# Sparse attention: the weighing factor of unit s+1 ahead of the low parts of unit s in VectorE's list

## The reference, cut to what matters

```
for head h (16), for m in (0: selected blocks, 1: window):
    s = (q_rope[h] @ k_m.T) * 64**-0.5          # 512 x 512, causal
    p = softmax(s)
    o[h] += sigmoid(gate_logits)[h, 1 + m] * (p @ v_m)
o[h] += sigmoid(gate_logits)[h, 0] * o_compressed[h]
```

## Time and profile before

| | us |
|---|---|
| median of 3 runs | 2101.65 (2101.18 to 2110.67) |
| the profiled execution | 2101.01 |
| its span in the profile | 2099.2 |
| first transpose of unit 0 to first transpose of unit 31 | 241.94 |

### The profile page before, as it was taken

How to read it: one execution, slowest core, us unless ns; L and a number is a source line. 1 busy time by engine, 2 the same in 40 slices (tenths; PEclk the granted TensorE clock), 3 DMA queues, 4 the chain that set the end, 5 groups by cost and what they waited for, 6 DMA issues and landing times.

```text
span 2099.2 us, 25667 instructions
## 1 busy us (share of the span) xinstructions
PE 2016.0 (96%) x10244; PEld 1696.5 (81%) x10244; DVE 1042.3 (50%) x1606; ACT 814.6 (39%) x1482; POOL 276.5 (13%) x272
## 2 busy tenths in 40 slices
PE   6999999999999999999998899989899999999998
PEld 6887888888888888888887688777777888888887
DVE  5675565555353222335545766766565543222333
ACT  5442443333343222324225744455554333222322
POOL 1001000000000000000012432376763000000000
PEclk9999999999999999999998999999999999999999
DMA  5231233333223333332541043212115423332332
GB/s 192 81 101 61 100 102 101 92 99 101 92 90 102 99 100 92 99 101 81 151 130 41 1 171 120 90 31 61 46 37 180 126 80 105 96 101 92 99 100 71
DMA packets 58982, 200.13 MB, mean 95 GB/s; under 512 B 8080, under 2 KB 8112, under 8 KB 58480
## 3 DMA queue, kind: packets, MB, share of 16 engines
q1 hardware_dynamic: 53936, 178.29, 27.1%
q0 software_dynamic: 4928, 20.21, 2.7%
HBM read 181.16 MB, written 8.39 MB: 90 GB/s over the span
## 4 chain that ended last, share of the span: by engine, by line
PE 76%; DVE 7%; POOL 5%; ACT 5%; issue 3%; DVEq 2%; DMA 1%; POOLq 1%; SPq 0%; ACTq 0%
PE ps L636 24%; PE ps L637 24%; PE ps L638 24%; POOL PU L592 5%; DMA raw<-in_w_all 1%; DVE Wl L1703 1%; DVE XN L1743 1%; PE ps L1089 1%; DVEq L2262 1%; POOLq L581 1%; PE ps L1005 1%; ACT Pb L1371 1%; ACT Wh L1210 1%; DVE AUl L2267 1%; ACT PL L1466 1%
## 5 line engine op out<-in xcount | busy, mean ns | idle before, releaser
L1703 DVE TENSOR_TENSOR Wl<-raw,Wh 128x1024 fp32r<-128x1024 f32 x307 | 378.3, 1235 | 754.1 <-ACT Wh L1210 752.7
L636 PE MATMUL ps<-HTh,Wh 128*128 128x512 f32 (+1 forms) x1728 | 647.4, 375 | 8.9 <-DVE HTl L1752 7.0
L638 PE MATMUL ps<-HTh,Wl 128*128 128x512 f32 (+1 forms) x1728 | 641.9, 371 | 0.0
L637 PE MATMUL ps<-HTl,Wh 128*128 128x512 f32 (+1 forms) x1728 | 641.6, 371 | 0.0
L1210 ACT CAST Wh<-raw 128x1024 fp32r<-128x1024 f32 x307 | 322.0, 1051 | 782.5 <-DMA raw<-in_w_all 782.5
L636 PEld LDWEIGHTS ps<-HTh,Wh 128*128 128x128 f32 x1728 | 327.5, 190 | 64.7 <-issue 9.7
L638 PEld LDWEIGHTS ps<-HTh,Wl 128*128 128x128 f32 x1728 | 327.0, 189 | 56.1
L637 PEld LDWEIGHTS ps<-HTl,Wh 128*128 128x128 f32 x1728 | 327.3, 189 | 54.0
L636 PE MATMUL ps<-Wh,Yh 128*128 128x512 f32 x528 | 205.8, 390 | 0.0
L638 PE MATMUL ps<-Wh,Yl 128*128 128x512 f32 x528 | 205.5, 389 | 0.0
L637 PE MATMUL ps<-Wl,Yh 128*128 128x512 f32 x528 | 205.4, 389 | 0.0
(11 more groups left out here) (281 smaller groups left out, 2370.0 us busy)
## 6 DMA issues: line engine op xcount, KB each, us to landing
raw<-in_w_all SPq DMA_DIRECT2D x307, 512.0 KB, 3.5
swp_d<-qkd SPq DMA_DIRECT2D x64, 64.0 KB, 2.7
g_dram<-gst SPq DMA_DIRECT2D x16, 256.0 KB, 4.0
ring<-g_dram POOLq DMA_DIRECT2D x16, 256.0 KB, 3.5
gpre<-in_g_pre POOLq DMA_DIRECT2D x5, 512.0 KB, 3.8
X<-in_x SPq DMA_DIRECT2D x4, 512.0 KB, 5.0
swp_r<-qkr SPq DMA_DIRECT2D x16, 128.0 KB, 2.3
cw1k<-in_cw POOLq DMA_DIRECT2D x1, 2048.0 KB, 8.6
```

The costliest lines, as they stand in the source:

```text
L636: tensor.matmul(dst, a_hi, b_hi, start=start, stop=False)
L637: tensor.matmul(dst, a_hi, b_lo, start=False, stop=False)
L638: return tensor.matmul(dst, a_lo, b_hi, start=False, stop=stop)
L1703: vector.tensor_tensor(Wl[:, s, :], raw[:, s, :], Wh[:, s, :], ALU.subtract).then_inc(w_lo, 1)
```

## The change

In VectorE's loop of the stage `nsa` the two calls change places. Nothing else in the program is different: no instruction is added or taken away, all semaphores and their values stay.

```
                 for s in range(32):
-                    unit_low(s)
                     if s < 31:
                         unit_gate(s + 1)
+                    unit_low(s)
                     if s and s % 2 == 0:
                         head_sum(s // 2 - 1)
                     if s < 30:
```

## The result

| | before | after |
|---|---|---|
| median, first set of runs | 2101.47 us (4 runs, 2101.18 to 2110.67) | 2077.45 us (4 runs, 2072.68 to 2085.32) |
| median, second set | 2106.21 us (18 runs, 2098.30 to 2109.58) | 2076.43 us (6 runs, 2070.75 to 2082.19) |
| span of the profiled execution | 2099.2 us | 2070.9 us |
| unit 0's first transposes to unit 31's | 241.94 us | 216.07 us |

The ratio is 0.9877 (95% interval 0.9853 to 0.9901) in the first set and 0.9868 (0.9846 to 0.9889) in the second: 1.2 to 1.3% faster, 24 to 30 us. The forecast was 2076.0 (2071 to 2088). Of the 28.3 us between the two profiled spans, 25.9 lie in the stretch that the change touches and 2.5 ahead of it, where the code is the same: unit 0's transposes began at 1347.08 us before and at 1344.61 after. Those 2.5 us are not from the edit.

A forecast was written before the change was run, and what follows sets the result against it. The prediction took the serial loop through VectorE's list as the bound (15.34 us a pair); 12 x 14.27, 2 x 13.5, 12.65 and 6.0 make 216.9 against 241.94, so 2101.0 - 25.0 = 2076.0 us, range 2071 to 2088.

The forecast's parts named there:

- The bound before: Units 0 to 31: low parts, factor, weighing in series through VectorE's list, 7.67 us a unit, 15.34 a pair.
- PE's pace: PE waiting for nothing: even unit 7.36 us, odd unit 6.91, full pair 14.27 against 15.34.
- The weighing in time: Split in even unit: weighing ends at 13.45, wanted at 14.27; split in odd unit: 1.7 us ahead of need.
- The short pairs: Pairs with a unit without a half: weighing binds, 13.5 us for (6, 7) and (22, 23), 12.65 for (14, 15).
- The sum: Unit 0's to unit 31's transposes: 171.2 + 27.0 + 12.65 + 6.0 = 216.9 us against 241.94, gain 25.0.
- The cross-check: PE's idle time 22.3 us, lower clock 2.5, modelled ends 5: 30 at most; less short-pair leftovers 2.0, 2.0, 1.1: 25.
- The shared resource: VectorE's low parts beside POOL's weighing: taken to cost 0, bounded by 1.08 us a unit; split beside idle POOL.
- PE is the bound already: Rival, whole stage: nothing moves, 2101 us; chance 0.04.
- Slower by the shared resource: Rival: split falls into the weighing, some 3.0 us on the chain, pair 16.5, time 2118; chance 0.03.
- another wait takes most of the gain: Rival: chain from low parts to weighing outgrows 0.8 us slack with split in even unit, 2080 to 2090; chance 0.12.
- The clock: Within main case: waits of 2.0 us at most could bring two dips to PE's lower clock, some 2 us each: 2080.

The follow-up runs named there:

- 6: Kernel before with one of three products left out in gate_half (8 matmuls a half instead of 12): ratio 1.0003, stage 241.94 us.
- 8: Kernel before with the weighing of the longest query tile (512 of 1280 columns) left out on GpSimd: ratio 0.9900, stage 220.1 us.
- 3: Changed kernel with the factor of unit s+1 moved behind the second of unit s's three low parts: ratio 0.9969 to the kernel before, stage 234.8 us.
- experiment 1: The changed kernel run once more, unaltered, with more runs: ratio 0.9868 to the kernel before, stage 214.41 us.
- 2: Changed kernel with the factor of unit s+1 moved behind the first of unit s's three low parts: ratio 0.9941 to the kernel before, stage 229.6 us.
- experiment 7: Changed kernel with one of three products left out in gate_half (8 matmuls a half instead of 12): stage 207.35 us.

## Why the prediction was right

**The bound before.** Shown: the loop through VectorE's list set the pace. It stays at 241.94 us with less PE work (6), gets faster with a cheaper weighing (8), and follows the place of the factor as the sum of its steps says, 7.35 us a unit behind two low parts (3). The stage before was 4.2 us longer than 15 pairs of 15.34 and a unit of 7.67: two dips made 3.1 of that, and units 5, 7 and 21 were 0.3 to 0.4 longer. That part of the gain is not from the shorter loop itself.

**PE's pace.** 14.27 us a pair were forecast, 14.10 to 14.11 came. The two units are 7.28 and 6.83 instead of 7.36 and 6.91: I had taken them from a unit whose transposes had waited, and those last 1.31 us instead of 1.25, which is most of it. Over the 12 pairs, some of which took 14.2, that is 1.6 us.

**The weighing in time.** The split in the even unit: forecast start at 9.18 and end at 13.45, 0.8 us to spare. After unit 4's transposes the weighing of unit 6 ran from 9.11 to 13.4 (it began at 1382.06), and its transposes came at 14.11, 0.7 us later. The short pairs took 13.32, 12.42 and 13.32 against 13.5, 12.65 and 13.5, the last unit 5.78 against 6.0.

**The sum.** 216.9 us were forecast and 216.07 came, of which a dip behind unit 23 made 1.6. So the terms without it were 2.4 us too long: 1.6 in PE's pace, 0.8 in the short pairs and the last unit. That the total came within 0.8 us is thus partly luck, and so is it that both medians lie within 1.5 us of 2076.0: the stage after began 2.5 us earlier for no reason of the edit, and in the second set the kernel before stood at 2106.21, so that the gain there was 29.8 us and not 25.0. The cross-check also left out a dip: PE was at a granted 0.50 from 1472.60 to 1475.60 as well, behind unit 15, and unit 16 took 8.84 us instead of 7.67. The way from unit 31's transposes to the next stage was 9.28 us (1560.68 to 1569.96), against 9.29 before:

```profile
1560.68 1.31 PE L1089 MATMUL ps<-ident,PU 128*128 128x128 f32 x10
...
1569.96 0.50 PE L636 MATMUL ps<-HTh,Wh 128*128 128x512 f32 x1 [0.59 <-DVE HTl L2324]
```

**The shared resource.** The unknown price was that of the low parts beside a weighing; 0 was taken of 0 to 1.08 us. The weighing's instructions have a mean of 1088 ns after and 1084 before (1091 with the one that ran beside a split), L2267 688 and 691: 0 was right. The split ended up beside an idle POOL, except in unit 0: there it started together with a query at 1351.26 us and took 1.23 us, and the query took 2.37 instead of 1.28 (in the profile of experiment 1 the split took 2.34 and the query 1.27). The pair took 14.24 us, PE waiting nowhere. All 19 splits between 1345 and 1595 us took 1.22 or 1.23 us. The factor's multiplication was held up as the rule of the Trainium skill says ("SBUF — State Buffer", section "Who interferes with whom"): five of 31 took 0.99 to 1.18 us instead of 0.17, each beside a query, as here in units 26 and 27. It cost nothing, since the weighing stands behind the queries anyway and PE waits for none of these:

```profile
1533.45 1.18 DVE L2263 TENSOR_TENSOR ugg<-ugg,gates 128x4 f32<-128x4 f32 x1
...
1533.33 1.28 POOL L584 TENSOR_TENSOR QSn<-qnr,QSn 64x512 fp32r<-64x512 f32 x1
```

**The rivals.** "PE is the bound already" is out by 6. "Slower by the shared resource" is out by the result, and "another wait takes most of the gain" did not happen in the changed kernel, but a collision can eat most of a pair's gain: 2 shows it, with 1.1 us a pair, when the factor stands one low part later. I had put the danger at the chain's length; it is the moment at which POOL's queries start. In the sum of the prediction this margin was there (queries end at 6.7, split at 7.5), and the trace has it (1379.5 and 1380.4, or 6.5 and 7.5 after the transposes).

**The clock.** PE fell to its lower level (1.2 GHz) behind unit 23 after a wait of 1.77 us. The forecast allowed for that at 2 us a dip; it cost 1.6:

```profile
1508.80:1510.90 2.10, 0.35 (x3) 0.14 (x2) 0.81 (x3) 2.00 (x8) 2.07 (x3) 1.00 0.00 0
1510.90:1515.00 4.10, 4.08 (x20) 3.40 (x20) 2.46 (x6) 2.03 (x4) 3.56 (x4) 0.59 0.01 2
```

The same wait behind unit 7, 1.77 us too, brought no dip (14.19 us for the next pair against 15.77 here), nor did either of them in experiment 1 (1.75 us each). What decides between them these runs don't show.

## What to carry to other kernels

An engine's share of the span doesn't tell whether an instruction list holds it up: find a stretch where the engine has less to do and see whether that stretch is shorter. If it isn't, follow the loop of waits once around, and look in each in-order list for a small instruction that depends on nothing near it but feeds the longest step. Put it as early as its own inputs allow, even at the price of a wait on the engine that has time; then look at which long instructions of VectorE and GpSimd now run at the same time, since a place that cuts the loop a little less can bring a collision that the better place avoids.

## What the runs showed of the hardware

- A VectorE subtraction with both inputs in SBUF (128x1024) takes 1.23 us alone and 2.25 us when a GpSimd instruction that reads SBUF has started 0.12 us before it; beside GpSimd memsets it takes 1.21 to 1.23. When the two start together either can be the one that stands: at 1351.26 us of the changed kernel's profile the GpSimd instruction took 2.37 us instead of 1.28 and the subtraction 1.23; in the profile of experiment 1 the subtraction, 0.01 us later than the other, took 2.34. A multiplication of 128x4 numbers, both inputs in SBUF, went from 0.17 to as much as 1.19 us (experiment 7).
- The start of the changed stage moved by 13 us with the same code ahead of it, and the granted clock moved with it. In two profiles, of experiments 1 and 3, unit 0 was transposed at 1344.35 and at 1357.69 us. The granted clock from 1150 to 1200 us was 1.00 in the one and 0.86 in the other:

```profile
1150.00:1200.00 50.00, 40.70 (x301) 33.76 (x300) 37.24 (x100) 37.75 (x118) 24.54 (x18) 1.00 0.01 1
```

```profile
1150.00:1200.00 50.00, 42.16 (x267) 34.41 (x266) 31.95 (x86) 32.10 (x101) 21.45 (x15) 0.86 0.00 1
```

In that stretch PE stands idle for 8 to 9 of 50 us anyway. All twelve profiles go this way (two of them have 16 matmuls fewer ahead of unit 0): from 1000 to 1300 us the clock was 0.98 in the seven with unit 0 at 1344.4 to 1347.1, 0.97 in the two at 1351, and 0.95 in the three at 1354.5 to 1357.7. That the clock makes the difference is not shown by itself. So one run of either kernel says little about an edit worth 1%, and the stretch from mark to mark says much.
